# Sparse attention on one core: the mask enters the logits' banks through TensorE instead of through VectorE

## The reference

```python
_, sel = lax.top_k(score, top_k)
valid = sel <= q_idx[None, :, None]
...
logits = jnp.einsum('bqgrd,bqkgd->bqgrk', q_b, k_sel, preferred_element_type=jnp.float32) * A_HEAD_DIM ** -0.5
logits = jnp.where(valid[:, :, None, None, :], logits, -jnp.inf)
p = jax.nn.softmax(logits, axis=-1)
o = jnp.einsum('bqgrk,bqkgd->bqgrd', p.astype(v.dtype), v_sel)
```

## Time and profile before

| | |
|---|---|
| median of three runs | 1252.22 us (1252.22 to 1253.5) |
| the profiled execution's own time | 1252.04 us |
| its span (first to last instruction) | 1250.3 us |
| TensorE busy | 1233.9 us, 99% |
| VectorE, ScalarE, GpSimd busy | 855.1, 593.5, 93.3 us |
| the attention units, first logits to last values | 67.3 to 93.5 us of the span |

### The profile page before, as it was taken

One profiled execution on the slowest core, in us unless ns is written; L12 is line 12 of the kernel. 1 busy time (PEld: TensorE's weight loads), 2 busy tenths in 40 slices (PEclk: granted clock), 3 DMA queues, 4 the chain that ended last, 5 costly groups with the idle time before them and its releaser, 6 DMA issues.

```text
span 1250.3 us, 19250 instructions
## 1 busy us (share of the span) xinstructions
PE 1233.9 (99%) x8277; PEld 1066.1 (85%) x8277; DVE 855.1 (68%) x919; ACT 593.5 (47%) x725; POOL 93.3 (7%) x226
## 2 busy tenths in 40 slices
PE   8989999999999999999999999999999999999998
PEld 7878888888888888888988888888998888888887
DVE  6787766666666676666786666667677667666675
ACT  5664443444744543443664543435563445434434
POOL 4351000001000200000201000001000100000000
PEclk9999999999999999999999999999999999999999
DMA  8423665565643755654624655555554347555542
GB/s 278 155 84 133 206 202 179 192 200 148 210 137 117 253 188 185 200 188 139 236 78 168 203 191 182 201 184 204 195 176 156 117 141 239 194 179 199 191 145 101
DMA packets 131268, 221.06 MB, mean 177 GB/s; under 512 B 6984, under 2 KB 99424, under 8 KB 131184
## 3 DMA queue, kind: packets, MB, share of 16 engines
q1 hardware_dynamic: 128160, 209.83, 50.1%
q0 software_dynamic: 3024, 10.01, 2.7%
HBM read 218.77 MB, written 1.05 MB: 176 GB/s over the span
## 4 chain that ended last, share of the span: by engine, by line
PE 90%; DVE 4%; DMA 2%; ACT 2%; POOL 1%; issue 1%; SPq 0%; POOLq 0%; DVEq 0%
PE ps L770 20%; PE ps L606 18%; PE ps L772 10%; PE ps L583 10%; PE ps L584 9%; PE ps L585 9%; PE ps L731 4%; PE ps L690 2%; PE ps L784 2%; DVE wlo L1796 2%; DMA raw<-in_mlp_w_up 1%; ACT whi L1338 1%; DMA raw<-in_ffn_w_in 1%; PE ps L941 1%; DMA raw<-in_a_w_in 1%
## 5 line engine op out<-in xcount | busy, mean ns | idle before, releaser
L1796 DVE TENSOR_TENSOR wlo<-raw,whi 128x2048 fp32r<-128x2048 f32 (+3 forms) x203 | 452.0, 2241 | 176.2 <-ACT whi L1338 175.3
L1338 ACT ACTIVATE whi<-raw 128x2048 fp32r<-128x2048 f32 (+3 forms) x203 | 377.1, 1870 | 70.9 <-DMA raw<-in_hgrn_w_in 21.1
L770 PE MATMUL ps<-xhl,whi 128*128 128x512 f32 x1088 | 271.4, 391 | 0.0
L770 PEld LDWEIGHTS ps<-xhl,whi 128*128 128x128 f32 x1088 | 198.3, 188 | 37.3
L606 PE MATMUL ps<-whi,xhl 128*128 128x512 f32 (+1 forms) x800 | 195.9, 377 | 2.4 <-DVE wlo L1796 1.5
L583 PE MATMUL ps<-whi,hh 128*128 128x512 f32 x432 | 169.0, 391 | 0.0
L584 PE MATMUL ps<-whi,hl 128*128 128x512 f32 x432 | 168.6, 390 | 0.0
L585 PE MATMUL ps<-wlo,hh 128*128 128x512 f32 x432 | 168.1, 389 | 0.0
L606 PEld LDWEIGHTS ps<-whi,xhl 128*128 128x128 f32 x800 | 140.4, 188 | 29.9 <-DVE wlo L1796 2.4
L772 PEld LDWEIGHTS ps<-xhl,wlo 128*128 128x128 f32 x1088 | 148.4, 190 | 10.6
L772 PE MATMUL ps<-xhl,wlo 128*128 128x256 f32 x1088 | 151.7, 282 | 0.0
(11 more groups left out here) (335 smaller groups left out, 1347.9 us busy)
## 6 DMA issues: line engine op xcount, KB each, us to landing
raw<-in_ffn_w_in SPq DMA_DIRECT2D x44, 1024.0 KB, 5.1
raw<-in_mlp_w_up SPq DMA_DIRECT2D x32, 1024.0 KB, 5.4
raw<-in_mlp_w_down SPq DMA_DIRECT2D x32, 1024.0 KB, 4.9
raw<-in_ffn_w_down SPq DMA_DIRECT2D x22, 1024.0 KB, 4.8
raw<-in_hgrn_w_in SPq DMA_DIRECT2D x16, 1024.0 KB, 5.3
raw<-in_b_w_in SPq DMA_DIRECT2D x12, 1024.0 KB, 5.3
raw<-in_ple_w_gate SPq DMA_DIRECT2D x8, 1024.0 KB, 6.0
raw<-in_a_w_in SPq DMA_DIRECT2D x6, 1024.0 KB, 5.5
```

Source lines behind the costliest of these rows:

```text
L770: mm(bank(b + f), w[0][:, kk, P * f : P * f + P], xhl[:, kk, :, :].rearrange("p a n -> p (a n)"), start=(kk == 0), stop=False)
L1338: a.activation(whi[:, slot, 0:w], raw[:, slot, 0:w], ACT.Copy).then_inc(s["hi_done"], 1)
L1796: v.tensor_tensor(wlo[:, slot, 0:w], raw[:, slot, 0:w], whi[:, slot, 0:w].bitcast(F32), ALU.subtract).then_inc(s["lo_done"], 1)
```

## The change

The bias is no longer added by VectorE. ScalarE copies it, rounded to the fp32r format, into a new tile `maskr` (and the identity matrix into `identr`), both in a part of `buf[2]` that is free by then. `logits(u)` begins with a product of `identr` and `maskr`, repeated over the heads by a broadcast, that writes the mask into the whole bank (one product of 512 columns for b = 0, two for b = 1); the four fp32 score products then accumulate on it. The scale of 1/8 moves to the copy of the transposed queries. VectorE's maximum and ScalarE's exponentials read the banks, and the exponentials write their result to the SBUF tile. With that a bank is free only when the exponentials have read it: `logits(u)` waits for `exp_done` of the unit two before it.

```diff
@@ TensorE, attention @@
                     if u >= 2:
-                        pe.wait_ge(s["logit_read"], u - 1)
+                        pe.wait_ge(s["exp_done"], u - 1)
+                    n = P * (b + 1)
+                    if u < TT:
+                        pe.wait_ge(s["mask_ready"], b + 1)
+                    mask = maskr[:, b, 0:n].unsqueeze(1).broadcast_to([P, 512 // n, n])
+                    for at in ((0,), (2, 3))[b]:
+                        mm(bank(at).rearrange("p (h n) -> p h n", n=n), identr[:, :], mask, start=True, stop=False)
                     for h in range(4):
-                        n = P * (b + 1)
                         last = score_mm(logit_out(b, h), b, 4 * g + h, n)
...
                     pe.wait_ge(s["exp_done"], u + 1)
-                    if u == n_units - 1:
-                        pe.wait_ge(s["logit_read"], u + 1)
...
-                return mm(o, qT[r, h // 2, b * P : b * P + P], kT[r, h // 4, h % 2, 0:n], start=True, stop=True)
+                return mm(o, qT[r, h // 2, b * P : b * P + P], kT[r, h // 4, h % 2, 0:n], start=False, stop=(h % 4 >= 3 - b))
@@ ScalarE, attention and what stands ahead of it @@
-                        last = a.activation(v, v, ACT.Exp, bias=negmax[:, u % 4, PLACE[b][h] : PLACE[b][h] + 1], accum_out=rowsum[:, b, 4 * g + h : 4 * g + h + 1])
+                        last = a.activation(v, logit_out(b, h), ACT.Exp, bias=negmax[:, u % 4, PLACE[b][h] : PLACE[b][h] + 1], accum_out=rowsum[:, b, 4 * g + h : 4 * g + h + 1])
...
             until(first["dsa_o"] + 1)
+            a.activation(identr[:, :], ident[:, :], ACT.Copy)
...
-                             ACT.Copy).then_inc(s["qT_done"], 1)
+                             ACT.Copy, scale=float(A_HD**-0.5)).then_inc(s["qT_done"], 1)
+                if hf == 1:
+                    act.wait_ge(s["bias_done"], tt + 1)
+                    a.activation(maskr[:, tt, 0 : P * (tt + 1)], bias[:, tt, 0 : P * (tt + 1)], ACT.Copy).then_inc(s["mask_ready"], 1)
@@ VectorE, attention @@
                     dve.wait_ge(s["logits"], u + 1)
-                    if u < TT:
-                        dve.wait_ge(s["bias_done"], b + 1)
...
-                    dst = logit4[u % 4][:, 0 : 4 * n].rearrange("p (h n) -> p h n", h=4)
-                    bb = bias_of(b)[:, 0:n].unsqueeze(1).broadcast_to([P, 4, n])
-                    v.scalar_tensor_tensor(dst, src, scale, bb, ALU.mult, ALU.add).then_inc(s["logit_read"], 1)
-                    dve.wait_ge(s["logit_read"], u + 1)
-                    v.tensor_reduce(negmax[:, u % 4, :], dst, AX_X, ALU.max, negate=True).then_inc(s["negmax"], 1)
+                    v.tensor_reduce(negmax[:, u % 4, :], src, AX_X, ALU.max, negate=True).then_inc(s["negmax"], 1)
```

More of the change, by code:

```diff
@@ L106, in build @@
         hl = nc.alloc_sbuf_tensor_at("hl", [P, 4, 512], F32R, offset=buf_home[6])
+        maskr = nc.alloc_sbuf_tensor_at("maskr", [P, TT, SEQ], F32R, offset=buf_home[2] + 4 * 1024)
+        identr = nc.alloc_sbuf_tensor_at("identr", [P, P], F32R, offset=buf_home[2] + 4 * 1536)
         ident = sb("ident", [P, P])
@@ L1930, in ffn, with attention @@
                     ahead(first[f"d{layer}.{g}"])
-            def attention(units, bias_of, scale, heads):
+            def attention(units, heads):
                 n_units = len(units)
@@ L2167, in _ @@
             v.tensor_copy(kvi[:, 1, FG : 2 * FG], bank(7, FG)).then_inc(s["v_dve"], 1)
-            attention(ATT_UNITS, lambda b: bias[:, b, :], float(A_HD**-0.5), A_HEADS)
+            attention(ATT_UNITS, A_HEADS)
             layer_norm(0, first["dsa_o"] + 3, T_X1)
```

## The result

The changed kernel takes 1254.7 us, the kernel before 1252.8 (medians of 21 runs each, 1253.7 to 1255.94 and 1251.28 to 1254.39). The ratio is 1.0017, 95% interval [1.0011, 1.0023]: slower by 1.4 to 2.9 us. The forecast was +0.8, so the loss is about two and a half times the forecast, and 1254.7 lies inside the predicted range. The profiled execution took 1254.61 us. In the runs of the kernel before that were timed beside the experiments, those with a mean granted clock of 1.0 take 1251.9 us (median of 41) and those with 0.998 or 0.999 take 1253.1 (median of 40), so about 1 us of a whole time does not come from the kernel.

A forecast was written before the change was run, and what follows sets the result against it. It took TensorE to bound the kernel, with VectorE on the attention's chain at both ends. Added masks less saved copies, carried through unit by unit, gave +0.8 us: 1252.8 profiled, 1253.0 us predicted median, range 1251.0 to 1255.4.

The forecast's parts named there:

- What bounds the attention: Attention, 26.20 us: the chain of waits runs through VectorE at start and end, TensorE alone from 74.35 to 85.24.
- VectorE's biased copies go, the maximum costs nothing more: Attention: VectorE saves 7.6 us over eight units; the maximum takes 1222 ns from a bank against 1221 from SBUF.
- The mask products, 0.235 each, ten on the chain: TensorE in the attention: 12 products of 512 columns at 0.235 us, 2.8 us in all, ten of them on the path.
- Exponentials from the banks: ScalarE in the attention: 480 ns instead of 500 for 256 columns, 20 ns less each, 0.08 us a unit.
- The scores of unit 3 come behind the wait, from unit 4 on no wait for exponentials: TensorE's logits: unit 3's 1.06 us of scores move behind the wait for exponentials; from unit 4 those are already over.
- The copies on ScalarE: Before the attention's first scores: the identity's copy costs nothing, the mask copies cost 0.1 us, at most 0.8.
- 1.88 us before the values of unit 5 shrink to about 0.7: Near the attention's end: TensorE's idle wait for VectorE's output falls from 1.88 us to about 0.7.
- The shift at the attention's end is the shift of the whole time, one for one: From the attention to the kernel's end: the +0.8 us at the last values reaches the whole time undiminished.
- nothing there is changed: Stretches outside the attention: none should move, so a gain beyond -1.9 us was unlikely; shifts elsewhere had chance 0.06.
- cheaper masks: Attention, rival: at 0.1 us a mask and 100 ns less per exponential, -0.9 us, 1251.3 us; chance 0.16.
- fp32 pace: TensorE's mask products, rival: 1.09 us per 512-column product, +9.4 us, 1261.6 us; chance 0.03.
- Exposed starts: Six later units, rival: each start on a handed-over bank exposed, masks 0.39 us each; +3.2 us, 1255.4 us; chance 0.13.

The follow-up runs named there:

- the doubled masks: The changed kernel with each mask product issued twice in a row into the same bank; ratio to the kernel before 1.0069 [1.0056, 1.0082], attention stretch 30.81 us.

## Why the prediction was right, and where it was not

- **What bounds the attention**: right. The chain runs where it was said to, through unit 1, TensorE alone, unit 7 and the output.
- **VectorE's biased copies go, the maximum costs nothing more**: right; VectorE's busy time fell by 7.1 us against 7.6, and a maximum of 1024 columns from the banks takes 1.22 to 1.23 us.
- **The mask products, 0.235 each, ten on the chain**: the rate is right (0.23 by the doubled masks), the term is mis-sized. A pair ahead of the scores that use half of the rows costs 0.2 more, for each of the four b = 1 units: 0.11 in its first product and 0.09 in the turn to the scores. That is 0.8 us on top of the 0.8 forecast, where 1.37 was measured. Of the 0.2 between, quicker exponentials explain about 0.1 by the prediction's own price for them; the rest was not traced. "10 of them behind the first unit" is a slip: eleven stand behind unit 0, and the sum counts the ten of units 1 and 3 to 7.
- **Exponentials from the banks**: direction right, size half. 476 ns with 256 columns against 480 forecast and 500 before; but one follows another after 0.45 us instead of 0.49, 0.04 less, twice what I took. The 0.04 is close to the 43 ns of the Trainium skill (VectorE: DVE Perf Modes, the section on the TRN2 errata for SBUF sources), and the measurement sides with it here.
- **The scores of unit 3 come behind the wait, from unit 4 on no wait for exponentials**: right, 0.90 us idle before unit 3's masks (1.0 was said), and none later.
- **The copies on ScalarE**: nearly free, as said. The masks of unit 1 start where unit 0's scores end, at 69.05.
- **1.88 us before the values of unit 5 shrink to about 0.7**: 0.63.
- **The shift at the attention's end is the shift of the whole time, one for one**: this step failed. At 911 us the changed kernel is 1.53 later, of which 0.46 was there before the attention, so the 1.37 us arrived as about 1.1; whether the missing 0.3 belongs to the scatter of the start is not shown. And 1.0 came on top from the fetch of TensorE's program. I had looked for what the attention passes on through semaphores and DMAs of weights, and left out that twelve more products move every instruction behind them. A sentence of the prediction ("nothing there is changed") is wrong in just this sense.
- **The rivals**: cheaper masks and fp32 pace fell. Exposed starts was the right direction with the wrong mechanism. From unit 4 on, taking over a bank costs nothing: from the start of the values to the mask behind them TensorE takes 0.62 us (76.85 to 77.47), as it took to the scores before (75.37 to 75.99). What costs is 0.2 for each pair of masks ahead of row-split scores.

So the forecast of no change by more than 0.2% held because the 0.8 forecast and two missed terms, 0.6 in the attention and 1.0 behind it, came to 2.4 us, just under it (2.6 us was measured in the profiled executions, with 0.46 of it from before the attention, and about 2 in the medians). That the second of them was no larger is luck: with other counts of instructions the same fetch cost up to 3.9 us.

## What to carry to other kernels

Moving work from VectorE to a busy TensorE pays only where VectorE's instruction stands on the chain: here for unit 7 alone, not for all eight. Whether it also pays for unit 1, whose copy stands on the chain too, was not tried. When a few instructions are added to an unrolled program, look for idle time with no releaser far behind the edit before you explain the whole difference by the edit. And test it with as many idle instructions at the start: one run tells the cost of the work from the cost of its place in the program. Look at the granted clock there too, since a gap may be followed by a stretch at half of it.

## What the runs showed of the hardware

- TensorE's instruction fetch can stall it. Here 24 or 48 instructions more, at the start or in the attention, open gaps of 0.85 to 1.9 us at bursts of 64 products with 16 columns, and 24 fewer close the one of the changed kernel. The gaps lie at fixed numbers of TensorE's program (product 6541 or 6542, and 2243 or 2244) and end 2.2 to 2.4 us after a transfer of the instruction queue began. The Trainium skill (Runtime: NRT & Kernel Launch, Instruction fetch mechanics) calls the cost of crossing a border of 16 KiB "mostly hidden"; it was hidden at nearly all 65 fetches of these traces, and not at one or two of them.
- After one such gap, of 1.59 us, the granted clock was 1.2 GHz instead of 2.4 for 3.4 us, and a product of 512 columns took 0.43 us instead of 0.23. After another, of 1.65 us, it was not.
- An fp32r product of 512 columns takes 0.23 us behind its like and 0.34 behind the products with the values; four fp32 scores of 128 columns that accumulate on it take 0.88 us instead of 0.99. A pair ahead of scores that use half of the rows costs 0.2 us beyond two times 0.23, 0.07 in bfloat16.
